# A transformer layer with attention, mLSTM and 32 experts on one core: x also sent transposed, q and k from unnormed rows, packed vectors, one mLSTM weight product, and 2 MB loads for three late experts

## The reference, cut to what matters

```
h = rmsnorm(x, norm1_g)
z = h @ w_in                     # q_a k_a v_a x_m v_m o_m: 512 columns each; i_pre f_pre: 4 each
qa = rmsnorm(heads(q_a, 8, 64), q_norm_g) * 64 ** -0.5
ka = rmsnorm(heads(k_a, 8, 64), k_norm_g)
attn = dilated_sliding_attention(qa, ka, va, slopes)      # 8 heads
xc = silu(causal_conv4(x_m))                              # 4 heads of 128
qm = einsum('bshd,hde->bshe', xc, w_mq)
km = einsum('bshd,hde->bshe', xc, w_mk) * 128 ** -0.5
hm = rmsnorm(mlstm(qm, km, vm, i_pre + b_i, f_pre + b_f), mh_norm_g)
x = x + concat(attn, sigmoid(o_m) * hm) @ w_out
x = x + moe(rmsnorm(x, norm2_g))     # router picks 4 of 32 experts for a token; 
                                     # each: 1024 -> 2 x 1024 (clipped swiglu) -> 1024
```

## Time and profile before

| | |
|---|---|
| median of 3 runs | 1052.33 us (1052.25 to 1052.73) |
| the profiled execution | 1052.36 us |
| its span | 1050.6 us |
| TensorE (PE) busy | 1035.1 us, 99% |
| VectorE (DVE) busy | 197.9 us, 19% |
| ScalarE (ACT) busy | 143.2 us, 14% |
| read from HBM | 423.31 MB, 404 GB/s over the span |
| time waited by TensorE for gate-up loads | 7.0 us |

### The profile page before, as it was taken

The page is one execution under the profiler, slowest core; times in us unless marked ns, Lnnn a source line. Parts: engine busy times, 40 slices in busy tenths (PEclk is TensorE's granted clock), DMA queues, the critical chain, the costliest instruction groups (busy, mean ns, idle before and its releaser), DMA issues.

```text
span 1050.6 us, 11670 instructions
## 1 busy us (share of the span) xinstructions
PE 1035.1 (99%) x4815; PEld 388.4 (37%) x4815; DVE 197.9 (19%) x500; ACT 143.2 (14%) x300; POOL 5.5 (1%) x23
## 2 busy tenths in 40 slices
PE   8999999999999999999999999999999999999998
PEld 4655543333333333333333333333333333333333
DVE  2162332111111111111111111111111111011111
ACT  2144431011111001101111111111101110011101
POOL 1000000000000000000000000000000000000000
PEclk9999999999999999999999999999999999999999
DMA  9964699999999999999999999999999999999996
GB/s 340 357 241 161 259 372 398 427 429 434 432 429 435 429 432 434 430 432 432 430 435 430 429 434 430 433 433 430 433 430 429 437 429 432 434 430 433 419 423 253
DMA packets 31519, 424.69 MB, mean 404 GB/s; under 512 B 5344, under 2 KB 6408, under 8 KB 15752
## 3 DMA queue, kind: packets, MB, share of 16 engines
q1 hardware_dynamic: 31192, 423.84, 95.5%
q10 hardware_dynamic: 304, 0.53, 0.1%
HBM read 423.31 MB, written 1.05 MB: 404 GB/s over the span
## 4 chain that ended last, share of the span: by engine, by line
PE 93%; DMA 5%; another core or an unknown queue 1%; DVE 0%; issue 0%; ACT 0%; SPq 0%
PE bank L1643 40%; PE bank L1678 19%; PE bank L1246 7%; PE bank L1605 5%; PE bank L1555 5%; DMA ring<-in_w_gate_up 5%; PE bank L1493 3%; PE bank L1440 3%; PE bank L1566 2%; PE bank L1663 2%; PE bank L1282 1%; PE bank L1654 1%; PE bank L1695 1%; PE bank L1394 0%; PE bank L1321 0%
## 5 line engine op out<-in xcount | busy, mean ns | idle before, releaser
L1643 PE MATMUL bank<-ring,xe_t 128*64 128x512 f32 x2048 | 448.1, 594 | 7.6 <-DMA ring<-in_w_gate_up 7.0
L1643 PEld LDWEIGHTS bank<-ring,xe_t 128*64 128x64 f32 x2048 | 143.6, 137 | 308.5 <-issue 294.1
L1678 PE MATMUL bank<-ring,late 128*64 128x512 f32 x992 | 219.9, 595 | 0.0
L1678 PEld LDWEIGHTS bank<-ring,late 128*64 128x64 f32 x992 | 68.4, 137 | 127.3 <-issue 123.5
L1165 DVE TENSOR_SCALAR gate_c<-bank 128x512 f32<-128x512 f32 x32 | 22.1, 692 | 434.7 <-PE bank L1643 434.7
L827 ACT ACTIVATE s_sb<-bank 128x256 f32<-128x256 f32 x32 | 12.3, 384 | 457.5 <-PE bank L1654 457.5
L1246 PE MATMUL bank<-ring 128*128 128x512 f32 x160 | 72.0, 596 | 0.5 <-issue 0.5
L1605 PE MATMUL bank<-late,s_sb 64*128 64x512 f32 x248 | 61.6, 615 | 0.0
L1555 PE MATMUL bank<-xres,pick 128*64 128x512 f32 x248 | 60.1, 605 | 0.0
L843 ACT ACTIVATE late<-bank 128x512 f32<-128x512 f32 x31 | 18.5, 597 | 218.8 <-PE bank L1678 218.8
L1163 DVE COPY row_of<-fold 128x64 f32 x31 | 6.0, 195 | 197.0 <-PE bank L1493 197.0
(11 more groups left out here) (214 smaller groups left out, 429.0 us busy)
## 6 DMA issues: line engine op xcount, KB each, us to landing
ring<-in_w_gate_up SPq DMA_DIRECT2D x50, 4096.0 KB, 36.9
ring<-in_w_down SPq DMA_DIRECT2D x25, 4096.0 KB, 35.4
ring<-in_w_gate_up SPq DMA_DIRECT2D x24, 2048.0 KB, 13.7
ring<-in_w_down SPq DMA_DIRECT2D x9, 2048.0 KB, 11.1
ring<-in_w_in SPq DMA_DIRECT2D x5, 2048.0 KB, 15.5
ring<-in_w_gate_up SPq DMA_DIRECT2D x8, 1024.0 KB, 24.1
ring<-in_w_down SPq DMA_DIRECT2D x6, 1024.0 KB, 29.1
ring<-in_w_out SPq DMA_DIRECT2D x2, 2048.0 KB, 10.4
```

The source lines that it names most:

```text
L1643: mm = pe.matmul(bank[h][c * CAP:(c + 1) * CAP, :], xe_t[:, k, :], w[:, k % RUN, at:at + BANK], start=False, stop=(k == KD - 1), skip_grou ...
L1678: mm = pe.matmul(dst[c * CAP:(c + 1) * CAP, :], turned[:, at:at + CAP], w[:, k % DRUN, c * BANK:(c + 1) * BANK], start=(k == 0), stop=(k = ...
```

## The change

It changes how inputs are laid out and in what order the front works; and it changes the size of loads for experts 27 to 29.

1. **x transposed.** The host passes x also as `x_t` (1 MB, [128, 8, 256]). ScalarE's queue loads it in three parts (slices 0, 1 to 2, 3 to 7) behind the vectors; SyncE's queue loads w_in's block 0 in the same parts, with nothing ahead. The halves of x follow behind block 1. DVE multiplies each slice by norm1_g (`xg`).
2. **q and k from unnormed rows.** Blocks 0 and 1 are multiplied with `xg`, both halves of tokens for each slice of block 0. Since q and k are normed by head afterwards, the 1/rms of the row drops out but for eps, which is replaced by eps * (mean square + eps) (`eps_x`). For the rest, 1/rms is spread over the partitions by two products (`rr` by identity), between the two halves of block 1, and DVE forms `ht` from `xg` by two multiplications. The squares of x on ScalarE come behind the squares of block 0.
3. **Packed vectors.** All gains, convolution weights and gate biases come as one array of 52 columns in one load; no transposition. w_in by blocks, w_out, the router with its bias, w_mq with w_mk and the gate columns (padded to 32) are laid out by partition, so that a partition's row in a load is contiguous.
4. **One mLSTM weight product.** scores = (xc w_mq)(xc w_mk)^T = (xc w_mq w_mk^T) xc^T: TensorE multiplies the two weights by head (4 products of 128x128) ahead of x_m; ScalarE copies the result (`wqk`). `project_m` runs once; km is gone, `m_score` takes xc.
5. **Rows in groups.** The fold products write each gate row on 32 partitions (128 in all), so the scans run on 128 partitions. The maxima are spread by four products, each on its own 32 rows, into banks 6, 3, 7 and 2. The columns of i and l are four full products, ahead of the attention loop. The first `attend` waits for all four decays.
6. **Experts 27 to 29 by 2 MB.** `PAIR_LAPS` is 11 instead of 12; experts 27, 28 and 29 are written out and loaded by `next_gu` and `next_d`. `add_residual` is thereby ahead of 27.

The diff, cut to its core:

```
-PAIR_LAPS = (NE - 3 - SINGLE) // LAP
+PAIR_LAPS = 11
+FINE = SINGLE + LAP * PAIR_LAPS
...
-    return SINGLE <= n < NE - 2
+    return SINGLE <= n < FINE
...
-            load_x(0)
-            sp.dma_start(win[:, 0, 0:2, :], w_in0[:, 0:2, 0:HALF]).then_inc(ld_win0[0], 16)
-            load_x(1)
-            sp.dma_start(win[:, 0, 2:4, :], w_in0[:, 2:4, 0:HALF]).then_inc(ld_win0[1], 16)
-            sp.dma_start(win[:, 0, 4:KD, :], w_in0[:, 4:KD, 0:HALF]).then_inc(ld_win0[2], 16)
-            sp.wait_ge(consts, 2)
-            sp.dma_start(wif[:, :, 0:2 * HM], w_in0[:, :, 6 * HALF:6 * HALF + 2 * HM]).then_inc(ld_wif, 16)
+            for i, (lo, hi) in enumerate(X_PARTS):
+                sp.dma_start(win[:, 0, lo:hi, :], w_in[0, :, lo:hi, :]).then_inc(ld_win0[i], 16)
             load_win(1)
+            for t in range(T):
+                load_x(t)
+            sp.dma_start(wif, w_if).then_inc(ld_wif, 16)
             load_win(2)
+            sp.dma_start(wm, w_m).then_inc(ld_wm, 16)
             load_win(3)
...
-            sp.wait_ge(qkm, 4)
+            sp.wait_ge(qkm, 2)
...
-                for n in range(SINGLE + LAP * PAIR_LAPS, NE - 2):
-                    next_pairs(base, 0, n)
+                for n in range(FINE, NE - 2):
+                    next_gu(base, n)
+                    next_d(base, n)
...
+            act.dma_start(vec[:, :], vecs).then_inc(ld_vec, 16)
+            for i, (lo, hi) in enumerate(X_PARTS):
+                act.dma_start(xg[:, lo:hi, :], x_t[:, lo:hi, :]).then_inc(ld_xt[i], 16)
...
+            for t in range(T):
+                square_z(t)
             for t in range(T):
                 act.wait_ge(ld_x[t], 16)
...
+            act.wait_ge(r_spread, 2)
+            act.activation(wqk, bank[5][:, :].rearrange("p (h n) -> p h n", h=HM), ACT.Copy).then_inc(qkm_read, 1)
...
+            for i, (lo, hi) in enumerate(X_PARTS):
+                dve.wait_ge(ld_xt[i], 16)
+                for k in range(lo, hi):
+                    dve.tensor_scalar(xg[:, k, :], xg[:, k, :], vec[:, R_G1 + k:R_G1 + k + 1], None, ALU.mult).then_inc(x_norm, 1)
...
+            squares_summed(0)
+            dve.wait_ge(x_rs, T)
+            dve.tensor_scalar(eps_x[:, :], ss1[:, :], EPS / D, EPS * EPS, ALU.mult, ALU.add).then_inc(rr_ready, 1)
+            for t in range(T):
+                dve.tensor_scalar(rr[:, t, :], ones[:, :], rs1[:, t:t + 1], None, ALU.mult).then_inc(rr_ready, 1)
+            dve.wait_ge(r_spread, 1)
+            for i in range(2):
+                dve.tensor_tensor(ht[:, 4 * i:4 * i + 4, :], xg[:, 4 * i:4 * i + 4, :],
+                                  bank[5][:, 0:SEQ].unsqueeze(1).broadcast_to([P, 4, SEQ]), ALU.mult).then_inc(h_ready, 1)
...
+            for i, (lo, hi) in enumerate(X_PARTS):
+                pe.wait_ge(ld_win0[i], 16)
+                for k in range(lo, hi):
+                    pe.wait_ge(x_norm, k + 1)
+                    for t in range(T):
+                        mm = project(bank[t], 0, t, range(k, k + 1), xg)
...
+            pe.wait_ge(ld_win[1], 16)
+            project(bank[2], 1, 0, tokens=xg).then_inc(z_q, 1)
+            pe.wait_ge(rr_ready, 1 + T)
+            for t in range(T):
+                mm = pe.matmul(bank[5][:, t * P:(t + 1) * P], rr[:, t, :], ident[:, :], start=True, stop=True)
+            mm.then_inc(r_spread, 1)
+            project(bank[3], 1, 1, tokens=xg).then_inc(z_q, 1)
...
+            pe.wait_ge(ld_wm, 16)
+            for m in range(HM):
+                mm = pe.matmul(bank[5][:, m * DM:(m + 1) * DM], wm[:, 0, m, :], wm[:, 1, m, :], start=True, stop=True)
+            mm.then_inc(r_spread, 1)
...
-                if j == 2:
-                    project_m(1)
...
-                        mm = pe.matmul(bank[6 + m // 2][:, (m % 2) * SEQ:(m % 2 + 1) * SEQ], sel[:, m, :], rows_a[:, :],
+                        rows = slice(m * NE, (m + 1) * NE)
+                        mm = pe.matmul(bank[A_AT[m][0]][:, A_AT[m][1]:A_AT[m][1] + SEQ], sel[rows, :], rows_a[rows, :],
                                        start=True, stop=True)
...
-                for n in range(SINGLE + LAP * PAIR_LAPS, NE - 2):
+                for n in range(FINE, NE - 2):
                     expert(base, 0, n, round_no)
```

More of the change, by code:

```diff
@@ L191, in layer_kernel @@
         mix_t = mix_flat.rearrange("p (k n) -> p k n", k=KD)
-        rows_i, rows_f, rows_l, rows_b, ones_r = (mix_flat[0:HM, i * SEQ:(i + 1) * SEQ] for i in range(5))
+        rows_i, rows_f, rows_l, rows_b, ones_r = (mix_flat[:, i * SEQ:(i + 1) * SEQ] for i in range(5))
         late = sb("late", [P, 2 * BANK])
         om = late[:, :].rearrange("p (t n) -> p t n", t=T)
+        sq_x = late[:, :]
+        rr = late[:, 0:T * P].rearrange("p (t n) -> p t n", t=T)
         bdn = late[:, 0:BANK]
@@ L263, in layer_kernel @@
         ld_x = [sem(f"ld_x{t}") for t in range(T)]
-        ld_g1 = sem("ld_g1")
+        ld_xt = [sem(f"ld_xt{i}") for i in range(len(X_PARTS))]
         ld_vec = sem("ld_vec")
@@ L956, in _ @@
+            squares_summed(1)
+            for s in range(2):
+                dve.wait_ge(qk_rs, s + 1)
+                for t in range(T):
+                    dve.tensor_tensor(qk_n[:, s, t, :].rearrange("p (h n) -> p h n", h=HA),
+                                      bank[2 * s + t][:, :].rearrange("p (h n) -> p h n", h=HA),
+                                      rsqk[:, s, t, :].unsqueeze(2).broadcast_to([P, HA, DA]),
+                                      ALU.mult).then_inc(qk_norm, 1)
             dve.wait_ge(z_if, 1)
@@ L1830, in expert_layout, with columns, by_partition, layout @@
     down[NE - 1, :, DN - 1] = last.reshape(P, DRUN, D)
-    return {"w_gate_up": gate_up.reshape(NE, 2, P, 2 * RUN, 2 * FF), "w_down": down.reshape(NE, P, DN * DRUN, D)}
+    return gate_up.reshape(NE, 2, P, 2 * RUN, 2 * FF), down.reshape(NE, P, DN * DRUN, D)
+def columns(given):
+    def by_partition(v):
+        return v.reshape(-1, P).T
+    qg, kg = (np.tile(given[n].reshape(DA), 2)[:, None] for n in ("q_norm_g", "k_norm_g"))
+    g2_run = given["norm2_g"].reshape(GUN, P, RUN).transpose(1, 0, 2).reshape(P, KD)
+    bi, bf = (np.repeat(given[n].reshape(HM), NE)[:, None] for n in ("b_igate", "b_fgate"))
+    parts = [by_partition(given[n]) for n in ("norm1_g", "norm2_g", "mh_norm_g", "conv_b", "conv_w")]
+    return np.concatenate(parts + [qg, kg, g2_run, bi, bf], 1)
+def layout(given):
+    w_in = given["w_in"][0].reshape(KD, P, -1).transpose(1, 0, 2)
+    w_if = np.zeros((P, KD, NE), np.float32)
+    w_if[:, :, 0:2 * HM] = w_in[:, :, 6 * HALF:6 * HALF + 2 * HM]
+    w_router = given["w_router"][0].reshape(KD, P, NE).transpose(1, 0, 2).reshape(P, KD * NE)
+    gate_up, down = expert_layout(given["w_gate_up"], given["w_down"])
+    return [("x", given["x"]),
+            ("x_t", given["x"][0].T.reshape(KD, P, SEQ).transpose(1, 0, 2)),
+            ("vecs", columns(given)),
+            ("w_in", np.stack([w_in[:, :, at:at + HALF] for at in IN_BLOCKS])),
+            ("w_if", w_if),
+            ("w_m", np.stack([given[n][0].transpose(2, 0, 1) for n in ("w_mq", "w_mk")], 1)),
+            ("w_out", given["w_out"][0].reshape(2, 4, P, D).transpose(0, 2, 1, 3)),
+            ("w_router", np.concatenate([w_router, np.broadcast_to(given["b_router"].reshape(1, NE), (P, NE))], 1)),
+            ("w_gate_up", gate_up),
+            ("b_gate_up", given["b_gate_up"]),
+            ("w_down", down),
+            ("b_down", given["b_down"]),
+            ("attn_bias", attention_bias())]
 def kernel(**inputs):
```

253 lines of the change are left out of this document (87 added, 166 removed).

## The result

The changed kernel takes 1053.53 us (1052.45 to 1055.55, 20 runs) against 1052.14 for the kernel before in the same rounds (1051.30 to 1052.74, 20 runs). The ratio is 1.0017, 95% interval [1.0011, 1.0023]: 1.4 to 1.8 us slower, under the 0.2% that the prediction calls no change, where 6.3 us faster was forecast. The profiled execution took 1053.87 us, its span 1052.1.

What follows compares the result with a forecast made beforehand. TensorE bounds the stretch before expert 0, the stream of loads that from expert 0 to 28, then TensorE again. Front 4.4 (2.0 + 1.73 + 1.27 - 0.54) plus end 1.9 gives 6.3 us gained: 1046.0, range 1043.6 to 1049.4.

Steps and rivals of the forecast that it cites:

- the failed step: Front: block 0's last part lands when 3.17 MB have moved, at 11.2 us (bounds 10.3 to 12.4).
- two queues share the DMA engines: Rival, chance 0.15: block 0's last part lands near 13.5, front less 2.3, 1048.3 us in all.
- slower: Rival, chance 0.03: block 0 waits for its parts, clock stays at 1.2 GHz until x_m, some 32 us; 1062 us.
- the 10.2 among my signs: Front: a wait of TensorE before the fourth slice of block 0, near 10.2 to 11.2 us.
- The sum up to x_m: Front: block 0 and the products behind it bring x_m's start to 36.1 against 38.1, 2.0 us gained.
- The slack I gave: Front, products of 1/rms: inputs ready 5.2 us after block 0, TensorE there after 7.0, slack 1.8.
- Attention: Front, attention: km product 1.73 us gained, spread of maxima 1.27 gained, columns of i and l 0.54 lost.
- Savings in front are kept whole: Time saved ahead of expert 0, 4.4 us, moves the issue of expert 2's first load and all landings with it.
- the rival in which the stream doesn't move with the front: Chance 0.03: the front's gain is lost or a new wait eats it; only the end's 1.9 stays, 1050.4 us.
- The end: Experts 27 to 31: waits of 27 and 28 go, 2.8 us; 0.9 of wait comes back; 1.9 gained (0 to 2.8).
- the slack at 31: Last expert: the third of the five last parts lands at 1039.1, TensorE needs it at 1041.8, slack 2.7 us.
- The 0.8 for the size itself: End: loads by 2 MB run at 428 GB/s against 432, 0.045 us for each of 18 pieces, 0.8 us.

Runs made afterwards that it cites:

- `e3_short_rows`: Changed kernel, both queues kept, with block 1 of w_in loaded by four loads of two slices (rows of 4 KB instead of 16); 1050.05 us.
- `e4_warm`: Changed kernel with 5, 2 and 9 more useless products in TensorE's waits ahead of slices 0, 1 and 3 of block 0; 1053.48 us.
- `e7_four_parts`: Changed kernel with x_t in SyncE's queue and block 0 with its x in four parts instead of three; 1046.33 us.
- `e5_end_alone`: Kernel before with only experts 27 to 29 written out and loaded by 2 MB; 1051.28 us.
- `e6_written_out`: Kernel before with experts 27 and 28 written out behind the loop but still loaded by pairs; 1052.67 us.
- `e2_one_queue`: Changed kernel with x_t issued by SyncE, each part just ahead of w_in's part, instead of on ScalarE's queue; 1048.61 us.

## Why the prediction was wrong

The forecast of 1046.0 failed in one step above all, and with it the sign. One queue alone brings the kernel to 1048.61, one queue and a finer last part to 1046.33 and 1046.47. That this is so near to 1046.0 is in part luck: the end gives less than forecast and attention more.

**When the last part of block 0 lands: the failed step.** The prediction took the bytes ahead of it (3.17 MB) over a rate and gave 11.2, at most 12.4. It landed at 16.80, and x_m started at 44.06, past the 38 that I had named as a sign of being wrong. The rate was right: 3.17 MB had moved by 11.2 in one queue, and 3.2 MB by 10.9 in the kernel after. Wrong was that these would be the bytes in front. Two things are in the 5.6. In one queue it lands at 12.96, outside my bounds too: I had let the bytes come strictly in the order of the queue, but 0.8 MB of the next block moves before the last byte of the part. I had row lengths only as a matter of rate, and misread them ("4 to 10 KB" leaves out x_t's), while between two queues they decided who moved on: x_t's 1, 2 and 5 KB stood against 10 and 16 KB, 184 packets with 0.30 MB against 181 with 1.70. TensorE's start of the part is 4.31 later than in one queue, and `e3_short_rows`, by cutting only the rows that run against x_t from 16 to 4 KB, takes 3.7 of the landing back. The rival "two queues share the DMA engines" (0.15) named what happened (from 5 to 10 us of the kernel after the queues have 85.5% and 16.9% of the engines' time) and mis-sized it: last part near 13.5, front less 2.3. It looked at the total, not at whose bytes pass first.

**The clock.** The rival "slower" gives it in GHz, which no run shows: the traces give the granted share, and at 0.50 four records took 3.41 us, against 1.75 at 1.00 (36 in 15.72). That a wait could bring the lower clock was my guess; the rows of before read 1.00 throughout. The rival had it last for 32 us. It did fall, but for 3.41 us and, if the mean clock of a run tells of it, only in half of the runs. These are 2.0 us slower, of which the 36 records show 1.6. The row I put against it was a wait of 1.36 between long bursts, and it had no fall (32 records in 7.09); waits of 2.38 (kernel after) and 2.15 (`e4_warm`) in a stretch with little before them had one, to 0.50. The clock comes second: the ten runs without a sign of a fall take 1052.70, still no gain. Of the 10.2 among my signs, 4.4 and 5.2 are start and products, and 0.6 is for a slow first slice, which no run of before shows. In the kernel after, the four records of that slice took 3.66, though the granted clock reads 1.00 there (the trace's first record of the clock is at 10.42 in the kernel after, so the 1.00 ahead of it is no reading); in `e4_warm` they took 1.95 behind twice as many useless products. It cost nothing, since the next part was not there yet.

**The sum up to x_m.** 36.1 was forecast, 44.06 came. Last part: 17.32 instead of 11.2, 6.1. Its 36 records 17.34 instead of 15.65 (18 products of 0.87): 1.7. From there to x_m 9.40, forecast 9.27 (0.43 + 6.96 + 1.00 + 0.88): 0.1. Together 7.9 of the 8.0. The durations of products at a granted clock of 1.00 were right: 0.87 for one of 512 columns, and for the small ones, where I counted 0.11 a record (0.22 for two at L1382), 0.44 for the four of the spreading and 1.09 for the eight of the weights, 0.2 over. The 0.22 a record in my bounds, as in the ten of the earlier trace rows in 2.21, did not come.

**1/rms.** The products that spread it follow at 34.50 without a wait. ScalarE finished it at 31.6, DVE's three operations follow. The slack I gave held. In `e7_four_parts`, where block 0 ends earliest, no wait shows there either.

**Attention.** Forecast 2.46 back; 2.99 came back between x_m and expert 2's first load. The spread took 0.65 for 1.92, its eight records in a third of the time, so four row groups did run side by side (that it is exactly the value I had picked between 0.4 and 1.0 is luck); the columns 0.79 for 0.34, 0.45 lost instead of 0.54; km is gone. These make 2.55. The other 0.4 lies ahead of attention: from x_m's first product to the end of the first turn of q it is 15.56 instead of 15.99, in x_m's products, the fold and the turn. I had put that stretch at nothing.

**Savings in front are kept whole.** Right in both directions, to 0.7: 2.94 late at the issue of expert 2's first load gives 2.38 late at expert 26; in `e7_four_parts` 4.27 early at the issue (forecast 4.4) gives 4.97 early at expert 26 (878.54) and 3.1 at the last landing, the rest being what part 6 costs there. So the rival in which the stream doesn't move with the front fell.

**The end: a mis-sized term.** The forecast was 2.8 won, 0.9 given back, 1.9 left; it is 0.6 to 1.2. What I named happened: waits at 24 to 26 stay, those of 27 and 28 go, a short one comes in the last expert. Given back are 0.40 at 29, 0.98 at 30 and 0.30 at 31, 1.7 in all. I saw only the slack at 31. The last landing moved 1.4 against the stream's start (4.32 less 2.94), and 1.9 from expert 26's first pair on (876.14 to the end, against 873.75), not 0.8. The 0.8 for the size itself nearly held: undisturbed, two loads of 2 MB take 9.79 and one of 4 MB 9.71, 0.7 for the nine pairs. The term that I had at nothing is the code: with experts 27 and 28 written out, the queue of instructions has three packets from 890 to 985 us instead of one, 0.2% of the time of the same 16 DMA engines instead of 0.1%, in a stretch where these are the bound (a share of 1.00). Each load that took longer landed within 5 us behind a fetch (954.78 behind 950.3, 980.21 behind 978.0), though not every fetch had such a load behind it (930.7 had none), and the delay is not the same each time: 0.4 and 0.9 here, 1.1 in `e5_end_alone` (948.40 behind 946.2), 1.6 in `e6_written_out`. The eighteen loads took 89.39 us, the same bytes before 87.74, fetches included. That the fetches are the cause goes by these times and by `e6_written_out`, in one trace of each kernel.

## What to carry to other kernels

Between two DMA queues, count packets, not bytes (here 181 and 184 packets stood for 1.70 and 0.30 MB): what TensorE needs first should be on one queue in the order of need, or have rows as long as what runs beside it (4 KB instead of 16 beside x_t's 5 took 3.7 us off its landing). Let the last part in front of a product be small, because here, in one queue, it landed at 12.96 where as many bytes had moved by 11.2: 0.8 MB of what is behind it moved ahead of its last byte. Where the stream of loads is the bound, look for the instruction fetches of code that you take out of a loop (here they went with landings about 1 us later), and a saved wait is only worth the slack of all later ones together, not of the last alone.

## What the runs showed of the hardware that was not expected

- Two queues with work had 181 and 184 packets in 5 us, with 1.70 and 0.30 MB: about one packet for one, whatever its size.
- In one queue, 3.17 MB had moved at 11.2 us, but the last byte of the first 3.17 MB landed at 12.96.
- Behind a wait of 2.38 us in a stretch of short bursts the clock was 0.50 for 3.41 us, and half of the runs have the mean clock that goes with it; in the profiles, waits of 1.59 and 1.40 had no fall behind them (1.00 from 13.0 to 16.0 in `e2_one_queue`, and from 885.89 to 889.00 in the kernel after).
- Two more instruction fetches, three for one from 890 to 985 us with the DMA engines at a share of 1.00, go with a last landing 0.77 later, 1.2 counted from expert 26's first pair.
- With 44 more records on TensorE early in the kernel, the last products stood 2.93 us without a missing operand; why is open.
